# Sums of weights in two chains between the heads, and a few instructions moved, in a fused two-layer kernel

## The reference

```python
h = rms_norm(x, g_pre_mix)
m = chunk_relpos_attention(h, w_qkv, w_o, rel_bias)   # 16 heads of 64, bias by distance
x = x + rms_norm(m, g_post_mix)                       # "post1" in the kernel
h = rms_norm(x, g_pre_ffn)                            # "pre1"
x = x + rms_norm((silu(h @ w_gate) * (h @ w_up)) @ w_down, g_post_ffn)   # F = 2816; "post2"
```

## Time and profile before

| | |
|---|---|
| median of 3 runs | 1370.99 us (1368.54 to 1374.07) |
| the profiled execution | 1370.99 us, span in the profile 1369.2 us |
| mean granted clock of TensorE | 0.963 |
| TensorE (PE) busy | 1262.5 us, 92% |
| DVE, ACT, POOL busy | 808.5, 625.1, 79.8 us |
| DMA | 250.06 MB, mean 183 GB/s |

### The profile page before, as it was taken

One profiled execution on the slowest core, in us unless ns is written; L12 is line 12 of the kernel. 1 busy time (PEld: TensorE's weight loads), 2 busy tenths in 40 slices (PEclk: granted clock), 3 DMA queues, 4 the chain that ended last, 5 costly groups with the idle time before them and its releaser, 6 DMA issues.

```text
span 1369.2 us, 18426 instructions
## 1 busy us (share of the span) xinstructions
PE 1262.5 (92%) x7031; PEld 1085.1 (79%) x7031; DVE 808.5 (59%) x1469; ACT 625.1 (46%) x1169; POOL 79.8 (6%) x133
## 2 busy tenths in 40 slices
PE   8999999104999999999999999999999999999998
PEld 7878777103989999988778888888887788898987
DVE  4367775004765455697766557776455543777664
ACT  4367665003454444555646432365235443463633
POOL 2100101111101000000011010000000000000000
PEclk9999999656999999999999999999999999999999
DMA  7999999875899855555534389722221122253541
GB/s 276 270 276 252 277 265 257 209 176 148 256 296 294 268 182 183 182 207 199 185 119 154 136 246 289 227 72 83 103 92 62 62 92 93 93 186 138 180 152 69
DMA packets 41704, 250.06 MB, mean 183 GB/s; under 512 B 5256, under 2 KB 6540, under 8 KB 14096
## 3 DMA queue, kind: packets, MB, share of 16 engines
q1 hardware_dynamic: 26952, 160.07, 32.8%
q0 software_dynamic: 11520, 83.89, 23.9%
q10 hardware_dynamic: 3144, 4.92, 1.1%
HBM read 240.46 MB, written 88.09 MB: 240 GB/s over the span
## 4 chain that ended last, share of the span: by engine, by line
PE 68%; DMA 24%; issue 3%; DVE 2%; ACT 2%; POOL 0%; ACTq 0%; SPq 0%; POOLq 0%; DVEq 0%
PE bank L2158 18%; PE bank L2160 18%; PE bank L2159 18%; DMA sum_dram<-in_weights 14%; DMA sum_dram<-sum_dram 7%; PE sc L2158 2%; PE sc L2160 2%; PE sc L2159 2%; DMA w_raw<-in_weights 2%; DVE w_lo L1346 1%; PE ob L2359 1%; PE sc L2335 1%; DMA w_raw<-sum_dram 1%; ACT w_hi L756 1%; PE tp L2344 1%
## 5 line engine op out<-in xcount | busy, mean ns | idle before, releaser
L1346 DVE TENSOR_TENSOR w_lo<-w_raw,w_hi 128x512 fp32r<-128x512 f32 (+1 forms) x427 | 331.3, 820 | 219.5 <-ACT w_hi L756 218.7
L756 ACT ACTIVATE w_hi<-w_raw 128x512 fp32r<-128x512 f32 (+1 forms) x427 | 287.5, 728 | 180.8 <-PE bank L2160 118.9
L2158 PE MATMUL bank<-xT_hi,w_hi 128*128 128x512 f32 (+1 forms) x960 | 352.1, 367 | 5.8 <-DVE w_lo L1346 2.3
L2160 PE MATMUL bank<-xT_hi,w_lo 128*128 128x512 f32 (+1 forms) x960 | 340.2, 354 | 0.0
L2159 PE MATMUL bank<-xT_lo,w_hi 128*128 128x512 f32 (+1 forms) x960 | 339.7, 354 | 0.0
L2158 PEld LDWEIGHTS bank<-xT_hi,w_hi 128*128 128x128 f32 x960 | 182.8, 190 | 33.7 <-issue 10.9
L2160 PEld LDWEIGHTS bank<-xT_hi,w_lo 128*128 128x128 f32 x960 | 182.5, 190 | 25.7
L2159 PEld LDWEIGHTS bank<-xT_lo,w_hi 128*128 128x128 f32 x960 | 183.1, 191 | 22.5 <-issue 1.2
L2158 PE MATMUL bank<-act_hi,w_hi 128*128 128x256 f32 (+1 forms) x288 | 95.8, 333 | 2.2 <-DVE w_lo L1346 1.9
L2159 PE MATMUL bank<-act_lo,w_hi 128*128 128x256 f32 (+1 forms) x288 | 95.1, 330 | 0.0
L2160 PE MATMUL bank<-act_hi,w_lo 128*128 128x256 f32 (+1 forms) x288 | 95.0, 330 | 0.0
(11 more groups left out here) (303 smaller groups left out, 2203.0 us busy)
## 6 DMA issues: line engine op xcount, KB each, us to landing
w_raw<-in_weights SPq DMA_DIRECT2D x94, 1024.0 KB, 5.0
sum_dram<-in_weights POOLq DMA_DIRECT2D x60, 1024.0 KB, 10.4
w_raw<-sum_dram SPq DMA_DIRECT2D x40, 1024.0 KB, 4.9
sum_dram<-sum_dram POOLq DMA_DIRECT2D x20, 1024.0 KB, 8.7
act_lo<-act_lo SPq DMA_DIRECT2D x24, 128.0 KB, 3.8
x_sb<-in_x SPq DMA_DIRECT2D x4, 512.0 KB, 6.9
w_raw<-in_weights SPq DMA_DIRECT2D x4, 512.0 KB, 9.0
arena<-in_bias ACTq DMA_DIRECT2D x16, 128.0 KB, 4.4
```

Of the source, the lines that this page charges most:

```text
L756: nc.scalar.activation(w_hi[SPLIT_AT[b]][:, cols], w_raw[SLOT[b]][:, cols], ACT.Copy)\
L1346: nc.vector.tensor_tensor(w_lo[SPLIT_AT[b]][:, cols], w_raw[SLOT[b]][:, cols], w_hi[SPLIT_AT[b]][:, cols].bitcast(F32), ALU.subtract).then ...
L2158: nc.tensor.matmul(ps, hi_l, hi_r, start=first, stop=False, skip_group_check=onto)
L2160: return nc.tensor.matmul(ps, lo_l, hi_r, start=False, stop=last, skip_group_check=onto)
```

## The change

- The ten groups become two chains: even groups on one pair of semaphores, odd ones on another. A double step is one step of each.
- POOL no longer fills the corners once. For each head it waits for the head's bias (now one transfer of the whole tile), fills the corner, signals `bias_ready`, and then makes `SUM_STEPS[h]` double steps: none for heads 0 to 3, two for each of heads 4 to 15. These are groups 0 to 7, all before `rstd` of `post1`. Groups 8 and 9 are made side by side where they were made in turn.
- DVE waits for `bias_ready` instead of for the bias and the corner.
- In a quad DVE's `split(up + 6)` goes ahead of `up_add(q, 4, ...)`.
- Near the end of the down phase two gains move from n = 12 to n = 16, and `update(1)` from n = 18 to n = 17, there ahead of `down_add(5)`. Around the last block before the second layer, the pieces of its split move among the norms of tiles 2 and 3, on ACT and DVE.

```diff
+SUM_STEPS = [0] * 4 + [2] * 12
...
-        corner_masked = sem("corner_masked")
+        bias_ready = sem("bias_ready")
...
-                    sp.wait_ge(*((pair_summed, 16 * (2 * g + 2)) if SUMS[n] == "pair" else (chain_summed, 16 * (6 * g + 2 * min(n, 2) + 2))))
+                    sp.wait_ge(*((pair_summed[g % 2], 16 * (2 * (g // 2) + 2)) if SUMS[n] == "pair" else
+                                 (chain_summed[g % 2], 16 * (6 * (g // 2) + 2 * min(n, 2) + 2))))
...
-            for place in biases:
-                nc.gpsimd.memset(place[0:CHUNK, BIAS_W - CHUNK:BIAS_W], NEG).then_inc(corner_masked, 1)
...
-                chain, pair_, k = chain_summed, pair_summed, g
+                chain, pair_, k = chain_summed[g % 2], pair_summed[g % 2], g // 2
...
+            def every_second(groups):
                 for g in groups:
                     yield from sums_of_weights(g)
...
-            add_weights(range(UP_QUADS + 1))
+            weight_sums = [every_second(range(i, len(GROUPS), 2)) for i in range(2)]
+
+            def add_weights(steps):
+                step_between(weight_sums[0], steps, weight_sums[1])
+
+            for h in range(HEADS):
+                pool.wait_ge(bias_loaded[h % 4], 16 * (h // 4 + 1))
+
+                nc.gpsimd.memset(biases[h % 4][0:CHUNK, BIAS_W - CHUNK:BIAS_W], NEG).then_inc(bias_ready, 1)
+                add_weights(SUM_STEPS[h])
             reciprocal_roots("post1", "pre1")
-            add_weights(range(UP_QUADS + 1, UP_QUADS + N_DOWN))
...
-            add_weights(range(UP_QUADS + N_DOWN, len(GROUPS)))
+            add_weights(6)
...
-                    for rows, cols in ((slice(CHUNK, P), slice(0, BIAS_W)), (slice(0, CHUNK), slice(0, BIAS_W - CHUNK))):
-                        act.dma_start(biases[h % 4][rows, cols], dram["bias"][h, rows, cols]).then_inc(bias_loaded[h % 4], 16)
+                    act.dma_start(biases[h % 4], dram["bias"][h, :, :]).then_inc(bias_loaded[h % 4], 16)
...
-                            dve.wait_ge(bias_loaded[h % 4], 32 * (h // 4 + 1))
-                            if t == 0 and h < 4:
-                                dve.wait_ge(corner_masked, h + 1)
+                            dve.wait_ge(bias_ready, h + 1)
...
+                split(up + 6)
                 up_add(q, 4, p5, 2, 2)
-                split(up + 6)
...
-                if n == 12:
+                if n == 16:
                     for t in range(2):
                         gain_down(t, 0, p1[:, t, :], p1[:, t, :], False).then_inc(gained, 1)
-                if n == 16:
                     for t in range(2):
                         gain_down(t, 1, u2[:, t, :], u2[:, t, :], True)
...
                 if n == 17:
                     update(0)
+                    update(1)
                 if n == 18:
-                    update(1)
                     scale("pre2", 0)
...
             gain_c21(2)
             variance("post2", 2, D)
-            step(parts, 2)
+            step(parts, 1)
             update(2)
-            step(parts, 1)
             gain_c21(3)
             variance("pre2", 2, D)
+            step(parts, 1)
+            scale_x("pre2", 2)
             variance("post2", 3, D)
-            scale_x("pre2", 2)
-            step(parts, 1)
+            step(parts, 2)
             update(3)
```

More of the change, by code:

```diff
@@ L449, in build @@
         left_made, down_full, down_copied, down_added, c21_free = (sem(n) for n in ("left_made", "down_full", "down_copied", "down_added", "c21_free"))
-        chain_summed, pair_summed = sem("chain_summed"), sem("pair_summed")
+        chain_summed, pair_summed = ([sem(f"{n}_summed{i}") for i in range(2)] for n in ("chain", "pair"))
         lhs_rounded, lhs_split = sem("lhs_rounded"), sem("lhs_split")
@@ L704, in sums_of_weights @@
                 yield
-            def sums_of_groups(groups):
+            def every_second(groups):
                 for g in groups:
                     yield from sums_of_weights(g)
-            def add_weights(groups):
-                step(sums_of_groups(groups), 6 * len(groups))
-            add_weights(range(UP_QUADS + 1))
+            weight_sums = [every_second(range(i, len(GROUPS), 2)) for i in range(2)]
[5 more added lines that the diff above has]
+                add_weights(SUM_STEPS[h])
             reciprocal_roots("post1", "pre1")
-            add_weights(range(UP_QUADS + 1, UP_QUADS + N_DOWN))
             reciprocal_roots("post2", "pre2")
@@ L732, in _ @@
                                         fill=ACAUSAL, base=0, pattern=[[-1, P]], channel_multiplier=1).then_inc(score_masked, 1)
-            add_weights(range(UP_QUADS + N_DOWN, len(GROUPS)))
-            pool.wait_ge(chain_summed, 16 * 6 * len(GROUPS))
-            pool.wait_ge(pair_summed, 16 * 2 * len(GROUPS))
+            add_weights(6)
+            for i in range(2):
+                pool.wait_ge(chain_summed[i], 16 * 6 * len(GROUPS) // 2)
+                pool.wait_ge(pair_summed[i], 16 * 2 * len(GROUPS) // 2)
             reciprocal_roots("final")
@@ L1066, in _ @@
             squares_c21(2)
-            step(parts, 2)
+            step(parts, 1)
             squares_x(2, 2)
-            step(parts, 1)
             squares_c21(3)
-            step(parts, 1)
+            step(parts, 3)
             round_xT("pre2", 2)
```

## The result

| | before | changed |
|---|---|---|
| median of 4 runs each, side by side | 1369.88 us (1368.54 to 1374.07) | 1453.06 us (1451.38 to 1453.32) |
| ratio, 95% interval | | 1.0599, 1.0573 to 1.0625 |
| the profiled execution, its span | 1370.99, 1369.2 us | 1452.84, 1451.1 us |
| mean granted clock | 0.963 | 0.938 |
| TensorE busy | 1262.5 us, 92% | 1293.3 us, 89% |

The change costs 83 us, 6.0%, by the medians, and 81.85 us between the two profiled executions. The forecast was 1464 us, inside a range of 1430 to 1505.

A forecast was written before the change was run, and what follows sets the result against it. TensorE was taken as the bound, except for an 81 us hole behind POOL's sums. Terms +77, -2.7, -7, +22.5, +1 and +2 summed to +92.8 on 1370.99 us: 1464 us, range 1430 to 1505.

The forecast's parts named there:

- part 3: Up-phase quads: the split ahead of the addition holds TensorE 4.5 us in each of five quads, +22.5 us.
- part 1: Heads 4 to 15: every head waits behind sums at 13.0 us a double step, delaying the transposes, +77 us.
- cold restart: Behind the present hole before the transposes: TensorE's slow restart there is gone, -2.7 us.
- part 2: Up phase: no sums run beside it any more, so late-load waits and lowered clock come back, -7 us.
- Part 4: End of the down phase: update(1) ahead of down_add(5) lengthens TensorE's wait, +1 us; moved split pieces taken at 0.
- Part 5: From 783 us: the last two groups side by side may delay some loads, +2 us.
- Part 6: Heads: bias in one transfer and a corner memset by POOL in each head cost nothing by themselves, 0.
- (a): Sums: two in flight overlap, a double step lasting 7.25 or 9.1 us; time 1343 or 1382 us; 5%.
- (b): Sums: a transfer costs no more than a load of weights, 3.0 us for 1024 KB; time 1405 us; 4%.
- (c): Sums: chains sharing a queue serialise, 18.2 us a double step, 1573 us; half way, 15 us, 1506 us; 8%.
- (d): Up quads: pace of the heads as forecast, but the addition's stall is hidden; time 1441 us; 8%.
- signs: Trace: 13 us double steps, heads 5 to 15 25 us apart, PE idle slices four to eleven, 4.5 us quad waits.

The follow-up runs named there:

- experiment 3: The changed kernel with split(up + 6) put back behind up_add(q, 4, ...); 1417.29 us, ratio 1.0328 to the kernel before.
- experiment 1: The kernel before with only split(up + 6) put ahead of up_add(q, 4, ...); 1400.77 us, ratio 1.0207.
- experiment 2: The kernel before with split(up + 6) ahead of up_add(q, 4, ...) and 36 unused matmuls filling TensorE's pause; 1386.16 us, ratio 1.0112.
- experiment 4: The kernel before with only the moves at the end of the down phase and among the last block's split pieces; 1370.36 us, ratio 1.0008.
- experiment 5: The kernel before with eight groups in two chains, all 24 double steps ahead of rstd, corners filled once; 1365.20 us, ratio 0.9963.
- experiment 6: The changed kernel with its two double steps a head in heads 0 to 11 instead of 4 to 15; 1451.84 us, ratio 1.0578 to the kernel before.
- four_groups_first: The kernel before, one chain, with only groups 0 to 3 ahead of rstd and groups 4 to 7 behind it; 1296.68 us, ratio 0.9471.
- four_groups_two_chains: The kernel before with two chains, 12 double steps ahead of rstd and 12 behind, heads free, corners filled once; 1320.56 us, ratio 0.9655.

## Why the prediction was right, and where it was off

The forecast was 1464 us, 11 us over the median of 1453.06. Its mechanism was the right one: every head waits for a corner that stands in POOL's queue behind sums which run at the pace of full DMA engines, and part 3 stalls TensorE in each quad. Two terms were mis-sized in opposite directions, part 1 by 20 us too much and part 3 by 10.5 too little, so that the sum lies as near as it does is partly luck.

**Part 1, the heads: +77 forecast, +57 measured.** Of the steps of that term:
- The start, 95 us by the forecast, is 87.4. The bias of head 4 is issued at 84.60 us instead of 90.73, and lands in 2.8 us, not 4. Without sums in that stretch the DMA share from 27 to 85 us is 0.41 in place of 0.90, and TensorE is busy for 58.0 of 58 us in place of 55.4. That is 7.6 us. I had read a time of issue from a stretch in which sums ran, and sums no longer run there.
- The pace, 13.0 us a double step, is 260.3 / 21 = 12.4, because the engines' share is 1.00 and not 0.96 and a transfer takes 3.93 us instead of 4.01. That is 12.7 us. The lower bound, a share of 1.0, was the truth. The other traffic took 14.6% of 260.2 us, 38 us (37 forecast).
- From the corner to the transposes 36.25 us (36 forecast). `rstd` adds nothing, as forecast.
- The sum 347.70 + 36.25 - 326.9 = 57.05.

**The cold restart and part 2, together -9.7 forecast, -10.9 measured.** Experiment 3 has both and no pauses: its up phase, from the transposes on, takes 244.5 us in place of 255.3 before.

**Part 3: +22.5 forecast, 33.0 measured in the up phase** (the changed kernel against experiment 3, whose medians are 35.8 us apart; alone in the kernel before 29.7, or 31 by the medians, experiment 1). The pause is as forecast, 22.6 us in five. The term left out the clock, 10.4 us: 2.5 us at the lower level behind the pause in which I counted the matmuls, 2.1 a quad on average, and 2.0 to 2.4 given back in undisturbed quads in experiment 2. In part 1, I had put that loss in for the hole; here I did not ask whether a pause of 4.5 us brings it too. Both bounds, 19 and 25 us, bounded the pause alone and missed the truth. The Trainium skill (TensorE: Matmul & The Clock Gate, "HAM oscillation — how this bites in real kernels") says that TensorE, stalled again and again by a wait, starts each burst at the lower clock, and prices it at half of the time spent there. The trace agrees in kind and nearly in size: 5.85 us at that level, of which half would be 2.9, and 2.5 lost.

**Part 4: +1 forecast, +2.7 between the two traces, 5.2 by the means of experiment 4.** TensorE's wait for the last `down_add` is 3.5 us instead of 2.3, which is the 1.2 us of the forecast; the rest comes behind it, among the norms and the pieces of the last block's split, which I had taken at 0. Which of these moves costs it is open. **Part 5: +2 forecast, 0.** The difference between the traces stays at 81.9 us from 718.43 us of the kernel before on, to the end, and the second layer takes the same time in every kernel, with the last two groups in turn or side by side. **Part 6: 0**, and one step of it is in the start of part 1.

Sum by what was measured in the traces: 57.05 - 10.9 + 33.0 + 2.7 = 81.85, the difference between the profiled executions. It closes by construction, since the stages follow each other; that the terms are rightly put down to their parts rests on experiments 1 to 4.

**The rivals.** (a), a double step of 7.25 or 9.1 us: it is 12.4. (b), a transfer at 3.0 us: it is 3.93, and the 2.4 us that the prediction worked out from the Trainium skill (DMA: Bandwidth & Descriptors, "Anatomy of one DMA — SWDGE (gpsimd) path") is further off still. (c), serialised chains at 15 to 18 us: the share of 1.00 leaves them no gap. (d), the stall hidden: five waits of 4.5 us. What I had named as signs came but for one: heads some 25 us apart (eleven in 260.3 us, 23.7 each, with ten waits of DVE for the corner, from head 6 on and not from head 5) and no wait for `rstd`. PE is low in the fifth to the tenth slice, not in the fourth to the eleventh.

**Where the 82 us between the traces come from, by kernels.** Eight groups in two chains for six in one, all ahead of `rstd`, heads free: -7 (experiment 5; -5 by the medians). The heads behind the sums: +51 (experiments 5 and 6). Part 3: +33. Part 4: +6 in this chain of kernels, +3 between the kernel before and the changed one. The late start of the sums: +1, no difference that can be measured. A rest of -2. The second item is work that ran beside the sums and now runs behind them. That the late start costs nothing surprised me; the start only matters where the heads could have been ahead of the sums.

## What to carry to other kernels

A queue in order carries its delay to whatever is put behind it: the corner's memset takes 0.15 to 0.45 us, and standing behind two double steps in each head it held DVE ten times, 155 us in all. Before spreading background transfers between steps of the work, add up their engine time (here 64 transfers of 3.93 us, 252 us) against the time of the steps (16 heads of 8.8 us, 141 us); if it is more, do fewer of them ahead of the next thing that is needed, as the two lines of `four_groups_first` do (-73 us), and leave the rest for later. And a pause of some microseconds on TensorE is priced with the slow restart behind it, here 6 to 7 us for 4.5.

## What the runs showed of the hardware

- After a pause of 4.5 us, TensorE's matmuls of 256 columns came every 0.21 us for 5.85 us, then every 0.12 us; with the pause filled by matmuls that nobody reads, they came every 0.12 us from the start, and the granted clock of the stretch was 1.00 instead of 0.94 (experiments 2 and 1, 460 to 520 us).
- A transfer of POOL's queue from DRAM to DRAM (half of them copies, half with addition) occupied all engines for 3.93 us at 1024 KB and 2.71 us at 512 KB.
- Two chains use what one leaves: the DMA share was 1.00 against 0.96 beside the heads. In exchange the 128 KB copies that double the keys (`act_lo<-act_lo`) landed in 8.6 us at the median in the changed kernel, 87.5 to 347.7 us (3.8 in the kernel before, 27 to 330 us). In `four_groups_two_chains` it was 9.6 us (27 to 250 us), and TensorE waited 8.4 us for such copies (`act_hi<-act_hi`).
- From one profiled execution to another, the second layer took 650.4 to 650.5 us in all twelve kernels, while the stage set by the transfers of the sums moved by 6.7 us (first transposes at 321.67 to 328.41 us in the four kernels that are the same up to there).
